# The vector c loaded as one row and spread over the partitions by TensorE, in place of some passes over zeros

## What is computed

```python
mod = c @ w_ada[l] + b_ada[l]
shift, scale, gate = jnp.split(mod, 3, axis=-1)
h = rmsnorm(x, norm_gain[l]) * (1.0 + scale[:, None, :]) + shift[:, None, :]
proj = h @ w_in[l]
...
h = h + ple_gate * (p[i] @ w_ple_proj[i])
```

## Time and profile before

| | |
|---|---|
| time, median of 3 runs | 1190.33 us (1190.3 to 1191.18) |
| span of the profiled execution | 1189.5 us |
| PE busy | 1167.8 us, 98% |
| PEld busy | 985.2 us, 83% |
| DVE busy | 757.3 us, 64% |
| ACT busy | 554.4 us, 47% |
| POOL busy | 97.3 us, 8% |
| HBM read, written | 178.52 MB, 52.43 MB |

### The profile page before, as it was taken

The page is one execution under the profiler, slowest core; times in us unless marked ns, Lnnn a source line. Parts: engine busy times, 40 slices in busy tenths (PEclk is TensorE's granted clock), DMA queues, the critical chain, the costliest instruction groups (busy, mean ns, idle before and its releaser), DMA issues.

```text
span 1189.5 us, 17906 instructions
## 1 busy us (share of the span) xinstructions
PE 1167.8 (98%) x7362; PEld 985.2 (83%) x7362; DVE 757.3 (64%) x1197; ACT 554.4 (47%) x886; POOL 97.3 (8%) x114
## 2 busy tenths in 40 slices
PE   7999999999999999999999989999999999999997
PEld 5887778788777887887777788889999999888886
DVE  6786555555567765548887785596767676444455
ACT  5425444536625445214547445465555555322254
POOL 0191011111000100100000200000000000100000
PEclk9899999999999999999999999999999999999999
DMA  9763279999721433992112101136655555633321
GB/s 375 290 205 113 67 261 313 243 271 327 180 71 54 133 111 117 336 244 67 54 59 84 36 4 37 48 113 215 219 181 183 179 194 173 239 98 98 102 87 73
DMA packets 57792, 185.97 MB, mean 156 GB/s; under 512 B 6544, under 2 KB 6672, under 8 KB 52592
## 3 DMA queue, kind: packets, MB, share of 16 engines
q1 hardware_dynamic: 47088, 127.29, 32.1%
q0 software_dynamic: 9776, 56.10, 17.3%
q10 hardware_dynamic: 848, 1.45, 0.3%
HBM read 178.52 MB, written 52.43 MB: 194 GB/s over the span
## 4 chain that ended last, share of the span: by engine, by line
PE 89%; DVE 4%; ACT 3%; issue 1%; DMA 1%; POOL 0%; ACTq 0%; DVEq 0%
PE pb L752 86%; PE pb L1015 1%; PE pb L843 1%; DMA aR<-a_spill 1%; DVE wlo L2059 1%; ACT Y L1501 1%; DVE xqs L2062 0%; DVE xT L2059 0%; DVE xlo L2059 0%; PE pb L1176 0%; ACT xhi L1501 0%; DVE tmpf L2059 0%; DVE ssq L2059 0%; ACT xq L1501 0%; ACT outT L1501 0%
## 5 line engine op out<-in xcount | busy, mean ns | idle before, releaser
L2059 DVE TENSOR_TENSOR wlo<-raw,whi 128x1024 fp32r<-128x1024 f32 (+1 forms) x210 | 254.8, 1215 | 112.9 <-ACT whi L1501 112.0
L752 PE MATMUL pb<-hhi,wlo 128*128 128x512 f32 (+2 forms) x696 | 271.1, 389 | 2.6 <-DVE wlo L2059 2.6
L752 PE MATMUL pb<-hhi,whi 128*128 128x512 f32 (+2 forms) x696 | 270.3, 388 | 0.0
L752 PE MATMUL pb<-hlo,whi 128*128 128x512 f32 (+2 forms) x696 | 269.0, 395 | 0.7 <-DVE tmpf L2059 0.7
L1501 ACT ACTIVATE whi<-raw 128x1024 fp32r<-128x1024 f32 (+1 forms) x210 | 214.6, 1037 | 84.1 <-DMA raw<-w_all 66.0
L752 PE MATMUL pb<-xlo,whi 128*128 128x256 f32 x616 | 174.9, 284 | 0.5 <-DVE xlo L2059 0.4
L752 PE MATMUL pb<-xhi,wlo 128*128 128x256 f32 x616 | 174.3, 283 | 0.0
L752 PE MATMUL pb<-xhi,whi 128*128 128x256 f32 x616 | 174.3, 283 | 0.0
L752 PEld LDWEIGHTS pb<-hlo,whi 128*128 128x128 f32 (+1 forms) x696 | 130.9, 188 | 30.6 <-issue 3.3
L752 PEld LDWEIGHTS pb<-hhi,wlo 128*128 128x128 f32 (+1 forms) x696 | 131.0, 188 | 30.3 <-DVE wlo L2059 3.5
L752 PEld LDWEIGHTS pb<-hhi,whi 128*128 128x128 f32 (+1 forms) x696 | 130.7, 188 | 27.3
(11 more groups left out here) (417 smaller groups left out, 1873.0 us busy)
## 6 DMA issues: line engine op xcount, KB each, us to landing
raw<-w_all SPq DMA_DIRECT2D x121, 512.0 KB, 4.2
w_sums<-w_all POOLq DMA_DIRECT2D x30, 1024.0 KB, 13.6
raw<-w_sums SPq DMA_DIRECT2D x88, 256.0 KB, 2.9
raw<-w_all SPq DMA_DIRECT2D x66, 256.0 KB, 3.1
w_sums<-w_sums POOLq DMA_DIRECT2D x10, 1024.0 KB, 11.0
adab<-ada_d SPq DMA_DIRECT2D x12, 512.0 KB, 11.8
gbt<-ada_d SPq DMA_DIRECT2D x12, 512.0 KB, 7.4
raw<-w_all SPq DMA_DIRECT2D x13, 384.0 KB, 3.1
```

The source lines that it names most:

```text
L752: return e.matmul(out, lhs, rhs, start=start, stop=stop, skip_group_check=True)
L2059: return e.tensor_tensor(out, a, b, op)
```

## The change

c is loaded as one row into partition 0 of `cbt`. DVE sets a row of 128 ones in `sq`. TensorE does 8 passes over zeros, waits for c, multiplies the ones (one partition by 128 columns) by the two halves of the row, which puts c on all 128 partitions of banks 5 and 6, and does 8 more passes. ACT copies the two banks to `cbt` ahead of its wait for p. `ada` waits for these copies instead of the transfer. The 20 passes have become 16.

```diff
+        CROW, CALL = sig("pe_crow"), sig("act_call", step=2)
...
-            e.dma_start(cbt[:, :], c_d.to_broadcast([128, D])).then_inc(CIN.sem, 16)
+            e.dma_start(cbt[0:1, :], c_d).then_inc(CIN.sem, 16)
...
             T.wait_ge(*EPSR())
-            for _ in range(20):
-                mm(PB[7][:, :], bcst[:, 0, :], bcst[:, :, :].rearrange("p a b -> p (a b)"), True, True)
+            def passes(n):
+                for _ in range(n):
+                    mm(PB[7][:, :], bcst[:, 0, :], bcst[:, :, :].rearrange("p a b -> p (a b)"), True, True)
+
+            passes(8)
+            T.wait_ge(*CIN())
+            for i in range(2):
+                t = mm(PB[5 + i][:, :], sq[0:1, 0, 0:128], cbt[0:1, 512 * i:512 * i + 512], True, True)
+            t.then_inc(CROW.sem, 1)
+            free[5], free[6] = [CALL()], [CALL()]
+            passes(8)
...
+            A.wait_ge(*CROW())
+            for i in range(2):
+                copy(cbt[:, 512 * i:512 * i + 512], PB[5 + i][:, :]).then_inc(CALL.sem, 1)
             A.wait_ge(*PIN())
...
-                V.wait_ge(*CIN())
+                V.wait_ge(*CALL())
...
             e.memset(bcst[:, :, :], 0.0)
+            e.memset(sq[0:1, 0, 0:128], 1.0)
             e.memset(epsc[:, 0:1], EPS)
```

## The result

The changed kernel takes 1195.89 us (median of 7 runs, 1194.74 to 1201.39) against 1190.33 (1188.73 to 1193.4); the ratio is 1.0049, with a 95% interval of 1.0032 to 1.0065. It is 5.6 us slower. The forecast was 4.4 us slower, 1194.7, in a range of 1191.0 to 1197.3.

The account below looks back on a forecast made before the run. TensorE, busy 1167.8 of 1189.5 us, was taken as the bound, so the start of its unbroken run counts. Copies and pair with their wait +5.4, slack -1.0, clock and rest 0: +4.4, so 1194.7; range 1191.0 to 1197.3.

Parts of the forecast that it names:

- The slack: At ACT's root of rsx, held by xn's landing: 1.0 us of the delay from the start is used up there.
- The landing: Row of c on POOL's queue: first packet about 5.6, TensorE's wait for it over at 6.5.
- Rival 1: Row lands by 4.65, so TensorE does not wait and goes to 2.4 GHz: 1191.3; chance 0.12.
- The pair: TensorE's two float32 products spreading c: four records some 0.86 us apart, ahead of every real product.
- ACT's order: ACT's two copies, 1.07 us together, stand ahead of everything in its queue: phi at 11.3, 5.4 us later.
- The run: TensorE's work without a break, starting at 29.75 before: starts at 34.2, the shift reaching the end in full.
- rival 4: Clock falls between the last passes and the first product, first groups slow: 1.4 to 2.8 us more, 1196.1 to 1197.5; chance 0.16.
- rival 2: Half-clock stretch in the bulk shrinks, up to 3.0 us come back: 1191.7 to 1193.2; chance 0.2.
- The clock of the bulk: Half clock from about 28.96 to 35.8 in TensorE's bulk: left at 0, bounds 3.0 us back or 1.5 more.
- the forecast's own 1193.4 to 1195.8: Range of the main forecast without the rivals, around its point 1194.7; chance 0.38.
- The traffic: Half a megabyte less to transfer: xn lands up to 1.25 us earlier, worth nothing by itself, only makes the slack usable.

Follow-up runs that it names:

- changed, second trace: The changed kernel's same code profiled and timed again; median 1197.8 against 1191.16, ratio 1.005.
- row by SP: Changed kernel with the row of c loaded by SP as its first transfer instead of by POOL; 1195.78 against 1191.4, ratio 1.0031.
- sixteen ahead: Changed kernel with 16 instead of 8 passes ahead of the wait for c; median 1196.7, ratio 1.0037.
- full rows: Changed kernel whose two products multiply 128 rows of ones by 128 rows of p, after c and p land; ratio 1.0039.
- before, eight passes: Kernel before the change with 8 instead of 20 passes over zeros, nothing else changed; ratio 1.0016.
- copies behind: Changed kernel with ACT's two copies behind phi and the first weights, without the 8 passes after the two products; ratio 1.0022.
- all three, 18 passes: Changed kernel with the row by SP, ACT's copies behind phi and first weights, 18 passes ahead, none after; 1191.15 against 1191.16, ratio 0.9999.
- all three, 12 passes: Changed kernel with the row by SP, ACT's copies behind phi and first weights, 12 passes ahead, none after; 1190.98 against 1191.17, ratio 1.0002.
- row alone: Kernel before with only the one-row transfer, no products or copies, 20 passes, ada multiplying each block by itself; ratio 0.9998.

## Why the prediction was right

One step of the sum, the slack taken off what the second `zs` copy is late, carries all traces. TensorE's run begins at 29.75, plus what the second `zs` copy is later than 12.42, minus the slack of 0.95 (that is, wherever xn's landing is no longer what the root waits for; in the kernel before it still is):

| kernel | phi | second zs | run by the rule | run measured |
|---|---|---|---|---|
| changed, first trace | 11.47 | 20.06 | 36.44 | 36.48 |
| changed, second trace | 11.41 | 17.87 | 34.25 | 34.31 |
| row by SP | 9.67 | 17.72 | 34.10 | 34.14 |
| sixteen ahead | 10.00 | 16.46 | 32.84 | 32.91 |
| full rows | 9.76 | 16.24 | 32.62 | 32.68 |
| before, eight passes | 6.03 | 14.48 | 30.86 | 30.90 |
| copies behind | 5.84 | 14.93 | 31.31 | 31.35 |
| all three, 18 passes | 4.79 | 14.72 | 31.10 | 31.14 |
| all three, 12 passes | 4.59 | 12.83 | 29.21 | 29.24 |
| row alone | 5.72 | 12.18 | 28.56 | 28.64 |

The measured run is 0.03 to 0.08 us above the rule each time, so the slack is 0.9 by the runs; from the second `zs` copy to the run it is 16.4 us in all ten. So whatever moves the start of the run lies ahead of the second `zs` copy. Point by point:

- **The slack** at the root was taken up and no more: 0.9 us, read as 1.0. Right.
- **The landing.** Predicted 6.5, the wait ended at 6.69 (5.4 from issue). The bound from the queue's first packet was the right row to lean on: the one-row transfer's first packets came in 5.5 to 5.75 as well. The transfer on POOL that took 2.7 us was the wrong neighbour. Rival 1 did not occur. The rule of the Trainium skill ("DMA: Bandwidth & Descriptors", section "Anatomy of one DMA — SWDGE (gpsimd) path") gave an estimate of 3.3 us for the moment when the row is there; the trace has 6.69.
- **The pair.** Predicted 3.44 at 1.2 GHz in four records, measured 3.77 with its end in both traces of the changed kernel, 3.78 in two others, and 1.98 at 2.4 GHz in four more. The count of two records for one float32 matmul decided this term: without it the pair would have been put at half.
- **ACT's order.** `phi` predicted 11.3, measured 11.47 and 11.41. The experiment that moves the copies, and drops the passes behind the pair with them, shows it as the largest single part that was tried.
- **The run** was predicted for 34.2. The second trace has 34.31. In the first, rival 4 came on top: half clock in the first products, 2.2 us, inside its 1.4 to 2.8; and rival 2 took 1.2 back.
- **The clock of the bulk**, which I left at 0, is the term that was not exact: in both traces of the changed kernel it gave back 1.2 to 1.35 us (100.54 and 100.42 against 101.77). The signs of the clock terms could not be had from one trace. So part of the closeness is luck: in the first trace 2.2 us of rival 4, 1.2 back from rival 2 and 1.3 behind the run make up 2.3 of the 2.4 between the forecast's 4.4 and the measured 6.8, and in the second the start and the bulk alone give 3.2. The mechanism up to the run is what was right.
- **The rivals** were priced one at a time, with chances that add up to 1. Rivals 2 and 4 came together, for which there was no place. The median of 1195.89 lies 0.1 us above the forecast's own 1193.4 to 1195.8 and inside the whole range, whose ends do not agree with the rivals that they are said to be: rival 1 gives 1191.3, not 1191.0, and rival 4 up to 1197.5, not 1197.3. Neither moves the result.
- **Behind the run** the sum had nothing. The wait of 0.4 us near 774 comes with the change and belongs into it.
- **The traffic**, worth nothing by itself in my sum, was worth 1.1 us of start when it stood alone, since without the delay its slack is usable. That agrees with the step, and it is the gain that the change gave away. Its size was read too low: the four loads of xn landed 10.6 us after issue (median) and not 12.4, 1.8 sooner where the sum allowed 1.25. Nothing hung on it.

What stays open is the share of each clock term in the median. Start and run explain 3.2 us (second trace, 134.73 against 131.53) to 5.5 us (first); by ratio the change costs 5.8 and 6.0. Executions also lose time later, as the second trace does near 725; five of twelve traces do, with and without the pair, which is too few to say how much of the median it is.

## What to carry to other kernels

Before work is moved to an engine at the start of a kernel, look at who stands behind it in that engine's queue: two short copies (1.1 us) placed ahead of the first real work carried their own wait for the landing and for the pair into all that followed, 5.5 us; behind it, nothing on the way to TensorE's run waited for them. A small transfer isn't early because it is small; the queue's first packet in the old trace tells when it can be there. Where a start is held by the landing of one transfer, the slack of the other chains against it, here 0.9 us, is both what a delay may use for free and all that a faster transfer can win.

## What the runs showed of the hardware

- **The clock at the start is not the same in every execution.** After the same eight passes and a pause of 1.7 to 1.8 us, the next products ran at 1.2 GHz in three traces (twice the changed kernel, and the one with the copies behind) and at 2.4 GHz in one (full rows). Behind nothing but passes, without a pause, the spacing went from 0.43 to 0.21 us at 4.58 (row alone), 5.05 and 5.41 (the kernel before, two traces), 5.60 (sixteen ahead) and about 7 (eighteen ahead). The Trainium skill ("TensorE: Matmul & The Clock Gate", section "What's actually happening") says that the number of matmuls which one kernel runs at the lower clock varies from run to run. The two traces of the changed kernel agree: the first products were 0.43 us apart in one and 0.23 in the other.
- **Around one-row products the clock was low more often than elsewhere.** With the row by SP, TensorE was busy from 1.36 to 12.18, the pair among it, and was still at 1.2 GHz at 13.1, behind a pause of 0.9; in the kernel before it rose at about 5.05, after 3.8 us. In the two versions with all three edits the clock fell shortly behind the pair (8.99 and about 10.5) with no pause ahead of it. But with sixteen passes ahead and eight behind it stayed up. Whether the single row is the cause was not tried by itself.
- **The granted clock reads 1.00 before its first recorded change**, also where the matmuls are 0.43 us apart.
- **POOL's first transfer starts late**: its first packets came 4.0 to 4.5 us after the issue, for 4 KB as for 512 KB, while SP's row, issued at 0.74, was there before 4.9.
